# The order of the first loads of a two-block transformer kernel: modulation rows first, key weights ahead of the gate's third

## The chip, the cores and the metric

The kernel runs on one NeuronCore of a Trainium2 chip. The metric is the device time of one execution in microseconds (us). Before the change the median of three runs is 2579.94 us.

## What is computed

Two transformer-like blocks in fp32 on x of 1024 tokens by 1024 features. Only the start of the first one matters here:

```
mod = c @ w_ada + b_ada                       # c: 1 x 1024, w_ada: 1024 x 3072
shift, scale, gate = split(mod, 3)            # 1024 each
h = rmsnorm(x, norm_g) * (1 + scale) + shift
proj = h @ w_in                               # conv inputs, q, k, v (24 heads of 64), gates
q, k = partial_rope(q), partial_rope(k)       # needs tables of cos and sin by position
...                                           # conv branch, three dilated window attentions, merge
x = x + gate * (merged @ w_o)                 # gate is used here for the first time
```

A second block with its own attention, pooling branch and a feed-forward part follows; nothing of it is touched.

## The kernel before

**Precision.** A projection in fp32 is done as three matmuls: operands are split into an upper part (hi, fp32r) and the rest (lo), and hi*hi, hi*lo and lo*hi are summed in one PSUM bank. A unit of projection, such as ("k", 0, 3), that is key, head group 0, token block 3, is 8 k-steps of three 128 x 128 x 512 matmuls, 24 in all. Weights come as pieces of 128 x 512 (256 KB) through four buffers `raw`; POOL splits each into `w_hi` and `w_lo` (L1067, L1069). The order of the units is written out by `plan`; four PSUM banks take them in turn, and ACT or DVE empties each.

**Engines and queues.** Each engine has its own program and waits on semaphores. SP issues nearly all DMAs in the order of its program, so a DMA that must wait for a free buffer holds back all that stand behind it. The eight blocks of x are issued by ACT. POOL does the weight splits of the whole first part, in order.

**The opening.** w_ada comes as 48 pieces of 128 x 512, named (n, k): n is which sixth of the 3072 columns, k which 128 rows. n = 0, 1 are shift, 2, 3 are scale, 4, 5 the gate. `ADA` is the order in which they are loaded. Two ways are used to multiply by c:
- n = 0 and 2: DVE multiplies a piece by c's column and adds it up (`ada_sum`, L1546 and L1549) in `macc`; at the end PE sums over the partitions and turns the result into columns of `ps_s[0]` (`mod_cols`, L2329). This gives the first half of shift and scale, for `mod_half(0)` on DVE and so the first four feature tiles.
- n = 1 and 3 ("row pieces"): PE multiplies c's column by the piece (`mod_piece`, L2336) into a row of PSUM. ACT copies the two rows out (L1165), and PE turns them into columns of `ps_s[1]` (`row_cols`, L2343) after the first k-step of the projections, for `mod_half(1)`.
- n = 4 and 5 (the gate): DVE sums as above in `gacc`; `gate_rows` (L2367) makes a row of it on PE, DVE adds the bias row `mrow` (loaded at L707), and `gate_store` (L711) writes the row to DRAM.

The pieces pass through a ring of 10 buffers (the first 32), later of 6 (the gate's 16), and SP waits at a piece until the piece before it in its slot was used (`ada_piece`, L687). Eight query weight pieces are issued between them (`next_piece`, L650), four at once and then one per split of POOL. The ring lies in `vreg` and `late_hi`; V of the attention is later written to `vreg`.

Per token block B, PE transposes x, already scaled by DVE (L1535), into `featT` (L2323, two sets of four transposes, copied by ACT at L1134). Before the change the row pieces lag two blocks: PE turns block B and then multiplies the row pieces of B - 2; behind the loop stand `mod_cols` for n = 0 and 2, and the row pieces of the last two blocks. Then DVE applies shift and scale to a feature tile of 128 x 1024 (`h_affine`, L1571), ACT takes its upper part (L1125), DVE its lower part (L1529), and the projections begin: four query units together, k-step by k-step, then one at a time.

**Rotation.** Behind h DVE computes the angles, ACT two tables by Sin (L1168, L1169; semaphore `rope_tab`). For each query and key unit ACT copies the bank (L1129), DVE rotates (four operations, L1630 to L1633), and PE transposes the result (`turn`, L2323), behind the next unit.

**Order on SP before the change.** 32 pieces with the queries' weights between them, the 16 gate pieces, the bias row, then `qkv_io`: one prefetch of a weight piece of the next chunk per unit (query units prefetch key weights, key units value weights). DVE sums two gate pieces behind each query rotation, `gate_rows` stands behind key unit 2, DVE's bias addition behind key unit 4, `gate_store` behind key unit 6.

Of the kernel before, what the change touches and what calls it, by code (L numbers as in the profile page):

```python
# [27 lines left out]
NB = S // P  # L28
KT = D // P
# [10 lines left out]
POOL_W = (2, 4, 8, 16)  # L40
ACC = 4
LEAD = 4
ROW_LAG = 2
ADA = ([(n, k - (ROW_LAG if n in (1, 3) else 0)) for k in range(8 + ROW_LAG) for n in (0, 2, 1, 3)
        if 0 <= k - (ROW_LAG if n in (1, 3) else 0) < 8]
       + [(n, k) for n in (4, 5) for k in range(8)])
ADA_SUM = {key: i + 1 for i, key in enumerate([key for key in ADA if key[0] not in (1, 3)])}
ADA_ROW = {key: i + 1 for i, key in enumerate([key for key in ADA if key[0] in (1, 3)])}
RAW = 4
# [4 lines left out]
FIRST_ADA = 32  # L54
ADA_SLOT = [p % RING if p < FIRST_ADA else (p - FIRST_ADA) % RING2 for p in range(len(ADA))]
ADA_BEFORE = [[q for q in range(p) if ADA_SLOT[q] == ADA_SLOT[p]] for p in range(len(ADA))]

# [153 lines left out]
def build(nc, A, out):  # L211
# [8 lines left out]
    with ExitStack() as ctx:  # L220
# [3 lines left out]
        def sem(name):  # L224
            return ctx.enter_context(nc.semaphore(name))
# [141 lines left out]
        ada_used, ada_col = sem("ada_used"), sem("ada_col")  # L367
        ada_mm, row_out, gate_b = sem("ada_mm"), sem("row_out"), sem("gate_b")
        gate_mm, gate_sum, gate_st = sem("gate_mm"), sem("gate_sum"), sem("gate_st")
        gs_ready, h_aff = sem("gs_ready"), sem("h_aff")  # L370
        ang_ready, rope_tab = sem("ang_ready"), sem("rope_tab")
# [41 lines left out]
        def wait_unit(eng, u):  # L413

            eng.wait_ge(acc_ready, U[u] + 1)

        def wait_evac(eng, u):

            eng.wait_ge(acc_free[U[u] % ACC], U[u] // ACC + 1)
# [218 lines left out]
        def _(sp):  # L638
# [40 lines left out]
            def ada_piece(p):  # L679
                n, k = ADA[p]  # L680
                if ADA_BEFORE[p]:
                    old = ADA[ADA_BEFORE[p][-1]]
                    if old in ADA_ROW:
# [16 lines left out]
            for p in range(8, 32):  # L700
                ada_piece(p)
                if p in (14, 16, 18, 20, 22, 24, 26, 28):
                    next_piece()
            for p in range(32, 48):
                ada_piece(p)
            sp.wait_ge(ada_col, 3)
            sp.dma_start(mrow, A["b_ada_row"][:, 2 * D:3 * D]).then_inc(gate_b, 16)  # L707

            def gate_store():
                sp.wait_ge(gate_sum, 2)  # L710
                sp.dma_start(gate_row_d, mrow).then_inc(gate_st, 16)  # L711
# [84 lines left out]
            def qkv_io(g):  # L796
                for u in STAGE_QKV[g]:
                    prefetch(u)
                    conv_io(u)
                    if u == ("k", 0, 6):  # L800
                        gate_store()

            for g in range(NG):
# [41 lines left out]
            for u in STAGE_Z:  # L845
                if u[0] == "zc":
                    n = GATES.index(u)
# [54 lines left out]
            n = 0  # L902
# [99 lines left out]
            for n in range(PRODUCTS):  # L1002
                blk, q = n // 7, n % 7
# [113 lines left out]
        def _(act):  # L1117
# [9 lines left out]
            def copy_unit(u, dst):  # L1127
                wait_unit(act, u)
                nc.scalar.activation(dst, bank(u), ACT.Copy).then_inc(free_of(u), 1)  # L1129
# [41 lines left out]
            def qkv_unit(u):  # L1171
                name, g, B = u
                if name in "qk" and g < NG:
                    wait_slot(act, u)
                    copy_unit(u, slot(u))
                elif name == "v":
                    if B == 0 and g >= 1:
                        act.wait_ge(pv, 16 * g)
                    copy_unit(u, V[:, B, :])
                elif name in ("qt", "kt"):  # L1180
                    if g >= 1 and g < NG and name == "qt" and B == 0:
                        act.wait_ge(scores, 64 * g)
                    wait_unit(act, u)
                    if g in (1, 2):
                        dst = (qT if name == "qt" else kT)[:, :, :]
                        src = bank(u)
                        if g == 1:
                            dst = dst.rearrange("p k (r h j) -> p k r h j", r=4, h=2)[:, :, :, B // 4,
                                                                                     32 * (B % 4):32 * (B % 4) + 32]
                            src = src.rearrange("p (k j r) -> p k r j", k=4, r=4)  # L1190
                        else:
                            dst = dst.rearrange("p k (r j) -> p k r j", r=8)[:, :, :, 16 * B:16 * B + 16]
                            src = src.rearrange("p (k j r) -> p k r j", k=4, r=8)
                        nc.scalar.activation(dst, src, ACT.Copy).then_inc(free_of(u), 1)
                    elif g == 3 and name == "kt":
                        nc.scalar.activation(kT2[:, P * B:P * B + P], bank(u)[:, 0:P], ACT.Copy
                                             ).then_inc(free_of(u), 1)
                    else:
                        transposed(u, (qT if name == "qt" else kT)[:, :, P * B:P * B + P])
                elif name == "kv":  # L1200
                    wait_evac(act, u)
                    nc.scalar.activation(V2[:, B, :], slot(("k", 3, B))[:, P:2 * P], ACT.Copy
                                         ).then_inc(v2_out, 1)
# [88 lines left out]
            for u in STAGE_Z:  # L1292
                name, B, h = u
# [218 lines left out]
        def _(dve):  # L1512
# [194 lines left out]
            for g in range(NG):  # L1707
                if g:
                    dve.wait_ge(probs_t, 32 * g)
                else:  # L1710
                    dve.wait_ge(rope_tab, 2)
                for u in STAGE_QKV[g]:
                    if u[0] in "qk":
                        wait_evac(dve, u)
                        rotate(u, HPG)
                    conv_taps(u)
                    if u[:2] == ("q", 0):
                        for p in (32 + 2 * u[2], 33 + 2 * u[2]):
                            ada_sum(*ADA[p])
                    if u == ("k", 0, 4):  # L1720
                        dve.wait_ge(gate_mm, 1)
                        dve.wait_ge(gate_b, 16)
                        for h in range(2):
                            nc.vector.tensor_tensor(mrow[:, HALF * h:HALF * h + HALF], ps_s[h][0:1, :],
                                                    mrow[:, HALF * h:HALF * h + HALF], ALU.add
                                                    ).then_inc(gate_sum, 1)
                attention(g)
# [73 lines left out]
            for u in STAGE_Z:  # L1801
                name, B, h = u
# [154 lines left out]
            for u in unit_range(("q", 3, 0), ("kt", 3, 7)):  # L1957
                name, _, B = u
# [242 lines left out]
            for n in range(PRODUCTS):  # L2201
                blk, q = n // 7, n % 7
# [43 lines left out]
        def _(pe):  # L2246
# [86 lines left out]
            def mod_piece(n, k):  # L2333
                p = ADA.index((n, k))
                pe.wait_ge(ada_ld[ADA_SLOT[p]], 16 * (len(ADA_BEFORE[p]) + 1))
                nc.tensor.matmul(ps_row[n], small[:, k:k + 1], ada[ADA_SLOT[p]], start=(k == 0),  # L2336
                                 stop=(k == KT - 1)).then_inc(ada_mm, 1)
# [11 lines left out]
            for i in range(2):  # L2349
                nc.tensor.matmul(ps_s[i][:, 0:16], ident[:, :], b_mod, start=True, stop=False, skip_group_check=True)  # L2350
            for B in range(NB):
                pe.wait_ge(x_norm, B + 1)
                for h in range(2):
                    turn(("xt", B, h), [xs[B % XS][:, P * i:P * i + P] for i in range(4 * h, 4 * h + 4)])
                if B >= ROW_LAG:
                    for n in (1, 3):
                        mod_piece(n, B - ROW_LAG)
            mod_cols(0, ps_s[0])
            mod_cols(2, ps_s[0])
            for k in range(NB - ROW_LAG, KT):  # L2360
                for n in (1, 3):
                    mod_piece(n, k)

            def gate_rows():
                pe.wait_ge(ada_used, ADA_SUM[(5, 7)])
# [57 lines left out]
            def attention(g):  # L2423

                us = att_units(g)
                for r in range(16):
                    a, b, c, d = four_fill(len(ATT_STAGES[g]), r)
                    for m in range(a, b):
                        proj(us[m // 24], m % 24)
                    score_four(g, r)  # L2430
                    for m in range(b, c):
                        proj(us[m // 24], m % 24)
                    turn_four(g, r)
                    for m in range(c, d):
                        proj(us[m // 24], m % 24)
                    value_four(g, r)
# [8 lines left out]
            for g in range(NG):  # L2445
                for u in STAGE_QKV[g]:
                    if u not in lead:
                        qkv_unit(u)
                    if u == ("k", 0, 2):
                        gate_rows()  # L2450
                wait_evac(pe, ("v", g, 7))
                attention(g)

            def turn_attention(B):
# [3 lines left out]
            for u in STAGE_Z:  # L2458
                name, B, h = u
# [112 lines left out]
```

## Time and profile before

| | |
|---|---|
| median of 3 runs | 2579.94 us (2577.8 to 2580.2) |
| profiled execution | 2578.96 us, its span 2576.8 us |
| busy share of the span | PE 97%, DVE 60%, ACT 33%, POOL 26% |
| mean granted TensorE clock | 0.993 |

The profile is of one execution. The span runs from the first instruction of the program to the end of the last; the execution's own time lies 2.2 us above it. Engines: PE = TensorE, PEld = its weight loads, DVE = VectorE, ACT = ScalarE, POOL = GpSimd, SP = SyncE; a q behind the name is the engine's sequencer, which issues DMAs. L687 is line 687 of the kernel. Times within the span are from its start. Matmuls are pipelined: one of 128 x 512 is recorded with about 0.39 us, but they start 0.23 us apart.

### The profile page before, as it was taken

The page shows a single profiled execution, that of the slowest core. Times are in us where ns is not written, and L with a number is a line of the kernel's source. Part 1 is how long each engine was busy: PE and PEld are TensorE (multiplying, and loading weights), DVE is VectorE, ACT ScalarE, POOL GpSimd, SP SyncE. Part 2 cuts the span into 40 slices and gives each one's busy share as a digit, 9 for nine tenths or more (in the row PEclk, how much of TensorE's full clock was granted, in tenths as well). Part 3 has the DMA queues.
Part 4 walks back from the last instruction along what each step waited for, and adds up shares of the span by engine and source line. Part 5 has one row for each costly group of instructions (what it writes and reads, how often), then busy time and mean ns, then how long its engine had stood idle before and what let it go on. Part 6 is the DMA issues. An engine that isn't in the chain of part 4 may idle for free.

```text
span 2576.8 us, 31389 instructions
## 1 busy us (share of the span) xinstructions
PE 2498.2 (97%) x12016; PEld 2052.6 (80%) x12016; DVE 1555.6 (60%) x2476; ACT 854.0 (33%) x1664; POOL 674.8 (26%) x653
## 2 busy tenths in 40 slices
PE   7999999999999999989999999999999999999997
PEld 4787887887888887778888888887887788887876
DVE  7511348978778686565646521123557866858778
ACT  5213221122321232463114033231145545354553
POOL 3422224323244232322533332223310000000000
PEclk9999999999999999999999999999999999999999
DMA  7311212213231232633434122215449575666754
GB/s 254 103 49 46 71 64 61 71 42 99 83 94 48 75 97 77 220 103 131 131 132 140 30 86 74 74 66 176 137 121 294 129 190 154 166 193 163 193 127 105
DMA packets 162794, 300.83 MB, mean 117 GB/s; under 512 B 22098, under 2 KB 46418, under 8 KB 158804
## 3 DMA queue, kind: packets, MB, share of 16 engines
q1 hardware_dynamic: 142724, 250.05, 29.3%
q0 software_dynamic: 18768, 44.57, 9.5%
q10 hardware_dynamic: 1152, 4.19, 0.4%
q8 instruction: 96, 1.57, 0.2%
q14 instruction: 54, 0.44, 0.1%
HBM read 232.50 MB, written 57.87 MB: 113 GB/s over the span
## 4 chain that ended last, share of the span: by engine, by line
PE 79%; DVE 12%; DMA 2%; ACT 2%; issue 2%; POOL 1%; SPq 0%; DVEq 0%; ACTq 0%; POOLq 0%
PE ps L2294 52%; PE ps L2520 19%; DVE scr L1650 5%; PE ps L2418 3%; PE ps L2394 2%; PE ps L2404 2%; PE ps L2323 1%; DVE w_lo L2034 1%; DMA h2c_d<-late_hi 1%; DVE w_lo L2043 1%; DVE big L2092 1%; DMA vreg<-in_w_ada 1%; DVE scr L1630 0%; DVE big L1890 0%; DMA late_hi<-in_w_ada 0%
## 5 line engine op out<-in xcount | busy, mean ns | idle before, releaser
L2294 PE MATMUL ps<-act_hi,w_hi 128*128 128x512 f32 x1344 | 540.0, 402 | 13.5 <-DVE act_lo L1529 4.1
L1067 POOL CAST w_hi<-raw 128x512 fp32r<-128x512 f32 x288 | 216.1, 750 | 1224.4 <-DMA raw<-in_w_in 776.3
L2294 PE MATMUL ps<-act_lo,w_hi 128*128 128x512 f32 x1344 | 534.7, 398 | 0.0
L2294 PE MATMUL ps<-act_hi,w_lo 128*128 128x512 f32 x1344 | 527.1, 392 | 0.0
L1650 DVE SCALAR_TENSOR_TENSOR scr<-scr,small 128x512 f32<-128x512 f32 x480 | 431.9, 900 | 15.6
L1069 POOL TENSOR_TENSOR w_lo<-raw,w_hi 128x512 fp32r<-128x512 f32 x288 | 402.8, 1399 | 23.1
L2294 PE MATMUL ps<-w_hi,act_hi 128*128 128x512 f32 (+1 forms) x960 | 377.2, 393 | 4.3 <-POOL w_lo L1069 2.6
L2294 PE MATMUL ps<-w_hi,act_lo 128*128 128x512 f32 (+1 forms) x960 | 369.9, 385 | 0.0
L2294 PE MATMUL ps<-w_lo,act_hi 128*128 128x512 f32 (+1 forms) x960 | 369.2, 385 | 0.0
L2520 PE MATMUL ps<-w_hi 128*128 128x512 f32 x896 | 350.6, 391 | 10.8 <-issue 7.7
L2520 PE MATMUL ps<-w_hi,w_lo 128*128 128x512 f32 x896 | 349.4, 390 | 0.0
L2520 PE MATMUL ps<-w_lo,w_hi 128*128 128x512 f32 x896 | 349.3, 390 | 0.0
L2294 PEld LDWEIGHTS ps<-act_hi,w_hi 128*128 128x128 f32 x1344 | 254.2, 189 | 74.6 <-issue 15.9
L2294 PEld LDWEIGHTS ps<-act_lo,w_hi 128*128 128x128 f32 x1344 | 253.6, 189 | 57.0 <-issue 4.6
L2294 PEld LDWEIGHTS ps<-act_hi,w_lo 128*128 128x128 f32 x1344 | 253.9, 189 | 50.2
L2294 PEld LDWEIGHTS ps<-w_hi,act_hi 128*128 128x128 f32 x960 | 198.1, 206 | 34.4 <-POOL w_lo L1069 3.9
L2294 PEld LDWEIGHTS ps<-w_hi,act_lo 128*128 128x128 f32 x960 | 197.8, 206 | 31.0
L1233 ACT ACTIVATE scr<-scr,stat 128x256 f32<-128x256 f32 (+1 forms) x256 | 115.9, 454 | 319.4 <-DVE stat L1672 319.4
L2294 PEld LDWEIGHTS ps<-w_lo,act_hi 128*128 128x128 f32 x960 | 198.4, 207 | 28.4
L2520 PEld LDWEIGHTS ps<-w_hi 128*128 128x128 f32 x896 | 168.5, 188 | 50.7 <-issue 15.9
L2520 PEld LDWEIGHTS ps<-w_hi,w_lo 128*128 128x128 f32 x896 | 168.6, 188 | 35.1
L2520 PEld LDWEIGHTS ps<-w_lo,w_hi 128*128 128x128 f32 x896 | 168.6, 188 | 34.7
(235 smaller groups left out, 2682.3 us busy)
## 6 DMA issues: line engine op xcount, KB each, us to landing
raw<-in_w_in SPq DMA_DIRECT2D x176, 256.0 KB, 3.3
late_hi<-h2c_d SPq DMA_DIRECT2D x21, 1024.0 KB, 7.5
vreg<-in_w_ada SPq DMA_DIRECT2D x36, 256.0 KB, 5.3
raw<-in_w_in SPq DMA_DIRECT2D x72, 128.0 KB, 2.4
raw<-in_w_up POOLq DMA_DIRECT2D x8, 1024.0 KB, 12.0
late_lo<-in_w_up SPq DMA_DIRECT2D x8, 1024.0 KB, 5.4
late_lo<-in_w_up POOLq DMA_DIRECT2D x8, 1024.0 KB, 15.8
late_lo<-late_lo POOLq DMA_DIRECT2D x8, 1024.0 KB, 7.4
```

Source lines behind the costliest of these rows:

```text
L1067: pool.tensor_copy(dhi, src).then_inc(w_hi_done, 1)
L1069: pool.tensor_tensor(dlo, src, dhi.bitcast(F32), ALU.subtract).then_inc(w_ready, 1)
L1233: nc.scalar.activation(p_, p_, ACT.Exp, scale=-1.0, bias=stat[:, B, h:h + 1], accum_out=stat[:, B, 8 + h:9 + h]).then_inc(probs, 1)
L1650: nc.vector.scalar_tensor_tensor(ca, u_in[:, j:j + HALF], w[:, j:j + 1], ca, ALU.mult, ALU.add).then_inc(tap, 1)
L2034: nc.vector.tensor_tensor(lo[:, two, :], src[:, two, :], hi[:, two, :].bitcast(F32), ALU.subtract).then_inc(wc_lo, 1)
L2043: nc.vector.tensor_tensor(lo[:, two, :], src[:, two, :], hi[:, two, :].bitcast(F32), ALU.subtract).then_inc(ac_lo, 1)
L2092: nc.vector.tensor_tensor(dst[:, t, :], dst[:, t, :], bank_, ALU.add).then_inc(signal, 1)
L2294: ins = nc.tensor.matmul(out_, lhs, rhs, start=(m == 0), stop=(m == 3 * nk - 1))
L2394: nc.tensor.matmul(ps_s[j][:, 256 * e:256 * e + n], qT[rows, i, P * B:P * B + P], keys, start=True, stop=True).then_inc(scores, 1)
L2404: ins = nc.tensor.transpose(ps_s[j][:, cols], prob[j][:, cols], ident[:, :])
L2418: ins = nc.tensor.matmul(ps_o[:, P * e + HD * j:P * e + HD * j + HD], prob[j][:, 256 * e + P * i:256 * e + P * i + P], v, start=(i == 0), ...
L2520: ins = nc.tensor.matmul(ps[prod_bank(n, t)][:, :], lhs, rhs, start=(k == 0 and i == 0), stop=(k == 3 and i == 2))
```

## The change

The order of the pieces loses its lag and puts the two row pieces of a k first. On PE the row pieces of a block precede its transposes. SP issues only gate pieces 32 to 37 in the opening, then the bias row, then waits for the rope tables; the other ten gate pieces are issued behind the prefetches of the first five key units. DVE sums two gate pieces behind each key rotation. `gate_rows`, the bias addition and `gate_store` move to value units 2, 4 and 6. Two waits are new: ACT waits for the last sum before it writes V, and PE for the gate's sum before the first attention.

```diff
-ROW_LAG = 2
-ADA = ([(n, k - (ROW_LAG if n in (1, 3) else 0)) for k in range(8 + ROW_LAG) for n in (0, 2, 1, 3)
-        if 0 <= k - (ROW_LAG if n in (1, 3) else 0) < 8]
+ADA = ([(n, k) for k in range(8) for n in (1, 3, 0, 2)]
        + [(n, k) for n in (4, 5) for k in range(8)])
...
@@ SP
                 ada_piece(p)
                 if p in (14, 16, 18, 20, 22, 24, 26, 28):
                     next_piece()
-            for p in range(32, 48):
+            for p in range(32, 38):
                 ada_piece(p)
             sp.wait_ge(ada_col, 3)
             sp.dma_start(mrow, A["b_ada_row"][:, 2 * D:3 * D]).then_inc(gate_b, 16)
+            sp.wait_ge(rope_tab, 2)
...
                     prefetch(u)
                     conv_io(u)
-                    if u == ("k", 0, 6):
+                    if u[:2] == ("k", 0) and u[2] < 5:
+                        ada_piece(38 + 2 * u[2])
+                        ada_piece(39 + 2 * u[2])
+                    if u == ("v", 0, 6):
                         gate_store()
@@ ACT, qkv_unit
                         act.wait_ge(pv, 16 * g)
+                    if B == 0 and g == 0:
+                        act.wait_ge(ada_used, ADA_SUM[(5, 7)])
                     copy_unit(u, V[:, B, :])
@@ DVE
-                    if u[:2] == ("q", 0):
+                    if u[:2] == ("k", 0):
                         for p in (32 + 2 * u[2], 33 + 2 * u[2]):
                             ada_sum(*ADA[p])
-                    if u == ("k", 0, 4):
+                    if u == ("v", 0, 4):
                         dve.wait_ge(gate_mm, 1)
                         dve.wait_ge(gate_b, 16)
@@ PE
             for B in range(NB):
+                for n in (1, 3):
+                    mod_piece(n, B)
                 pe.wait_ge(x_norm, B + 1)
                 for h in range(2):
                     turn(("xt", B, h), [xs[B % XS][:, P * i:P * i + P] for i in range(4 * h, 4 * h + 4)])
-                if B >= ROW_LAG:
-                    for n in (1, 3):
-                        mod_piece(n, B - ROW_LAG)
             mod_cols(0, ps_s[0])
             mod_cols(2, ps_s[0])
-            for k in range(NB - ROW_LAG, KT):
-                for n in (1, 3):
-                    mod_piece(n, k)
...
-                    if u == ("k", 0, 2):
+                    if u == ("v", 0, 2):
                         gate_rows()
                 wait_evac(pe, ("v", g, 7))
+                if g == 0:
+                    pe.wait_ge(gate_sum, 2)
                 attention(g)
```

## Rows read from the trace of the kernel before

**Rows 1.** The page: the chain that ended last, shares by engine.
```profile
PE 79%; DVE 12%; DMA 2%; ACT 2%; issue 2%; POOL 1%; SPq 0%; DVEq 0%; ACTq 0%; POOLq 0%
```

**Rows 2.** Stages: length, busy us by engine, granted PE clock, DMA share, GB/s.
```profile
10.00:20.00 10.00, 5.84 (x25) 3.66 (x24) 5.71 (x11) 7.37 (x15) 0.00 (x0) 0.80 1.05 368
...
30.00:40.00 10.00, 7.67 (x30) 2.44 (x29) 9.39 (x12) 3.29 (x7) 9.68 (x9) 1.00 1.05 387
```

**Rows 3.** Timeline of SP, 37 to 82 us: start, length, instructions merged.
```profile
37.24 44.63 SPq L687 DMA_DIRECT2D vreg<-in_w_ada  x18
```

**Rows 4.** Line 687, the issue at 37.7 us: lengths in ns, starts, landing.
```profile
L687 SPq DMA_DIRECT2D vreg<-in_w_ada x1: 430/430/430, 37.7 to 37.7; - x1
...
DMA to landing us min/median/max: 5.5/5.5/5.5
```

**Rows 5.** Timeline of PE, 9 to 47 us; brackets: idle before, releaser.
```profile
9.43 3.48 PE L2323 MATMUL ps<-ident,scr 128*128 128x128 f32 x16 [3.27 <-DVE scr L1535]
...
18.44 3.57 PE L2336 MATMUL ps<-late_hi,small 128*1 128x512 f32 x4 [1.74 <-DMA late_hi<-in_w_ada]
...
35.62 1.09 PE L2323 MATMUL ps<-ident,scr 128*128 128x128 f32 x8
...
39.70 1.95 PE L2329 MATMUL ps<-small,vreg 128*128 128x1 f32 x16
...
43.29 1.88 PE L2336 MATMUL ps<-vreg,small 128*1 128x512 f32 x4
46.78 0.47 PE L2294 MATMUL ps<-w_hi,act_hi 128*128 128x512 f32 x1 [1.61 <-DVE act_lo L1529]
```

**Rows 6.** Chain of waits, 41 to 47 us: start, length, what.
```profile
41.95 1.48 DVE big L1571
43.45 1.07 ACT act_hi L1125
44.54 2.10 DVE act_lo L1529
```

**Rows 7.** Timeline of DVE, 46 to 49 us.
```profile
46.55 0.80 DVE L1571 TENSOR_SCALAR big<-big,col 128x1024 f32<-128x1024 f32 x1
47.27 1.22 DVE L1529 TENSOR_TENSOR act_lo<-big,act_hi 128x1024 fp32r<-128x1024 f32 x1
```

**Rows 8.** Chain of waits, 80 to 120 us.
```profile
80.76 0.77 DVE scr L1549
...
82.29 4.63 DMA raw<-in_w_in
...
102.50 1.60 POOL w_lo L1069
...
105.31 0.85 PE ps L2323 x4
106.17 6.44 PE ps L2294 x24
112.61 0.44 PE ps L2323 x4
113.05 5.47 PE ps L2294 x24
118.52 1.81 PE ps L2367 x4
```

**Rows 9.** Timeline of PE, 94 to 96 us.
```profile
95.52 0.60 PE L2323 MATMUL ps<-ident,scr 128*128 128x128 f32 x4
```

**Rows 10.** Waits on PE, 86 to 113 us: total us, times, longest.
```profile
PE ps L2294 <- POOL w_lo L1069: 2.6, 2, 1.7
```

**Rows 11.** Timeline of ACT, 67 to 69 us.
```profile
67.75 0.40 ACT L1169 ACTIVATE cosT<-scr 128x256 f32<-128x256 f32 x1
```

**Rows 12.** Timeline of DVE, 90 to 97 us: first rotation operation, two sums.
```profile
90.50 0.54 DVE L1630 TENSOR_TENSOR scr<-scr,cosT 128x128 f32<-128x128 f32 x1 [3.37 <-ACT scr L1129]
...
93.55 2.82 DVE L1549 SCALAR_TENSOR_TENSOR scr<-vreg,small,scr 128x512 f32<-128x512 f32 x2
```

## The prediction

> **What bounds the kernel now.** I read four views: the page with its chain of waits, the table of stages, then the chain and the timelines of the first 120 us, since every edit lies there. The page puts 79% of the chain on PE [rows 1]: past the opening the work is a train of matmuls, and whatever removes idle PE time ahead of it, or adds some, moves the end by the same amount. So two places matter.
>
> *The opening, 0 to 46.8 us.* The DMA engines are full, 368 GB/s from 10 to 20 us and 387 from 30 to 40 [rows 2]. A 256 KB piece then takes 262144 B / 387 GB/s = 0.68 us, and pieces land one behind another. SP hands the last modulation pieces and all the gate's pieces to the queue in one stretch of 18 from 37.24 on, 44.63 us long [rows 3]. The last modulation piece ahead of the gate's third is issued at 37.7 and is 5.5 us under way, so it lands at 43.2 [rows 4]. Yet PE forms the columns of shift and scale at 39.70 [rows 5], before the last pieces have landed: they are row pieces, which only the second half of the columns needs. From there it is DVE's affine, ACT's upper part (1.07), DVE's lower part (2.10), and the first projection at 46.78 after 1.61 us of idle PE [rows 5, 6].
>
> *The key weights, 80 to 113 us.* In that stretch of SP's queue the gate pieces from the seventh on wait for a slot that a sum beside a query rotation frees, and the key weights stand behind them. The chain shows it: a sum on DVE at 80.76, the first key piece in flight from 82.29 for 4.63, POOL's splits from then to 104.10, and only then the last matmuls of the first key unit. Behind it the clock fell to its lower level, 1.2 GHz: four transposes took 0.85 instead of 0.44 us, and a unit of 24 matmuls 6.44 instead of 5.47 [rows 8].
>
> **Part 1: key weights are asked for behind the rope tables.** SP now issues gate pieces only up to the sixth, loads the bias row, waits for the two tables and then prefetches keys. The second table is written by 68.15 [rows 11]; with the opening's shift (part 3) that is 70.2. The first key piece then needs 2.5 to 4.6 us (4.63 is the one row of it, with four pieces in the queue) and is in by 75. Eight splits took 104.10 - 86.92 = 17.2 us with a busy DVE beside them, so the last is ready by 92. The first key unit is due at 96.1 + 2.3 = 98.4: 6 us to spare, the stall is gone whole. Its size: from the transposes behind the last query unit at 95.52 [rows 9] to the third key unit at 113.05 is 17.53 us. The work in it is three transposes of 0.44 and two units of 5.47, as the next ones run [rows 8]: 12.26. So **-5.3 us**, the low clock included. Bounds: -2.6 (only PE's two waits for POOL [rows 10]) to -5.3. I take the full value, since the gap between the two is short gaps at the same matmuls and the low clock behind them.
>
> What it adds: POOL's splits now run from 75 to 92 under the query rotations. A rotation beside POOL took 93.55 - 90.50 = 3.0 us, with the first sum right behind it [rows 12]. Each has a unit of 5.47 us as cover from its copy to its transpose, and the sums are gone from beside it. The first, which has no such cover, comes at about 72, before POOL starts. Price nothing; if the cover failed, up to 3.0 us per unit.
>
> **Part 2: the gate's sums move beside the key rotations, the gate's row into the value units.** Sixteen sums leave the query stretch, where they were not on PE's path except through SP, and join the keys: rotation 3.0 + two sums 2.82 = 5.8 us with POOL active throughout [rows 12], against a unit's period of 5.91. POOL has only one value piece per key unit (1.9 us), so about 4 us of 5.9. SP is new in this stretch: behind each of the first five key prefetches it waits for that unit's sums before it can ask for the next value piece. The fifth key unit ends at 98.4 + 4 x 5.91 + 5.5 = 127.5, its sums at latest 6.4 later, 133.9; the last three value pieces, with two gate pieces ahead of them, land some 5 us later, by 139, and take 3 x 2.15 = 6.5 on POOL, 145.5. The first value unit starts at 98.4 + 8 x 5.91 = 145.7, and needs its last piece only 4.8 us later. Covered. ACT's first copy into V now waits for the last sum, at most 6.4 us behind the last key unit against 5.9 for the value unit itself: 0.5 us late on one of four banks, free. The two gate matmuls cost PE 1.81 us where they stand [rows 8], between key units before, between value units after: the same. The wait for the gate's sum ahead of attention is met units earlier. Part 2 is **0**; bounds 0 to +3.5 (the value weights as late as the keys' were, 9.0 for a unit of 5.47).
>
> **Part 3: the opening.** All eight input blocks load the same bytes, and the SP waits that hold issues back from 24 us on are on POOL's splits, whose places in the queue are unchanged. So I let the last piece land at 43.2 again. But it is now the second scale piece, on which DVE's sum, and with it the first columns, depend, and the two row pieces before it stand ahead of the last block's transposes on PE. Two chains:
> - DVE: 43.2 + sum 0.77 + columns of one piece 1.95 / 2 = 45.0.
> - PE: the second row piece lands two pieces before the last, 43.2 - 2 x 0.68 = 41.8; its matmul 1.88 / 2, the two sets of transposes 1.09, both columns 1.95 [rows 5]: 45.8.
>
> The later one counts: 45.8, against 39.70 + 1.95 = 41.65 now, 4.1 us later. Part of it comes back: from 46.5 on affine and lower part took 0.80 and 1.22 [rows 7], against 1.48 and 2.10 for the first ones, which ran beside POOL's last query splits [rows 6]. Mine come behind those splits: 45.8 + 0.3 + 0.80 + 1.07 + 1.22 + 0.1 = 49.3, against 46.78: +2.5. POOL too may be quicker where DVE waits for pieces, and then the pieces land up to 1 us sooner: half of that off. **+2.0 us**; bounds +0.8 to +3.6 (all of it off and no contention; DVE and POOL slowing each other as now).
>
> **Part 4: the clock at the start.** PE now idles from 45.8 to about 49. Before, it idled 1.61 us there and the clock stayed at 2.4 GHz, by the first matmul's 0.47 [rows 5]; behind the 2.6 us of waits around 103 [rows 10] it fell, and cost 0.41 + 0.97 [rows 8] and some 0.3 at the matmuls ahead of these, 1.7 in all. My idle is longer than either, but of a kind seen once each way: even chances at 1.7 us, **+0.9**; bounds 0 to +3.4 (it falls twice).
> The Trainium skill, page "TensorE: Matmul & The Clock Gate", section "HAM oscillation — how this bites in real kernels", says that a wait for data between bursts re-throttles the array and the next burst begins cold, each time anew. By it the sum would be 0.8 us higher than by the row of 46.78, at which a short wait cost nothing.
>
> **Sum.** -5.3 + 0 + 2.0 + 0.9 = -2.4. The profiled execution took 2578.96 us, of which the span is 2576.8: 2576.6. The median of the runs shown is 1.0 above that execution, so 2577.5 beside it. Of the chances: a change under 0.2% (5.2 us) can't be told from none with this kernel.
>
> **Rivals.**
> 1. *The opening costs nothing* (13%). The row pieces, now spread over all blocks, keep the clock up, DVE is idle more often, POOL gets ahead, and the last pieces land two us sooner. For it: PE ran at 0.80 of its clock from 10 to 20 us [rows 2]. Against: the DMA engines are full, whatever the order. It gives -5.3 + 0.1: 2574.7.
> 2. *PE becomes the bound of the opening* (6%). If the clock stays at its lower level, a row pair takes 3.57 and a block's transposes 3.48 / 2 [rows 5], 5.3 us per block on PE, and each now blocks the next; DMA needs 5 x 0.68 = 3.4. The third block's first row piece lands 31 pieces before the last, 43.2 - 31 x 0.68 = 22.1; six blocks from there end at 53.9, the columns at 55.9, the first projection 3.5 later at 59.4, +12.6. That would be 2579.9 - 5.3 + 12.6 = 2587.2, slower than before. It decides if the clock is low for more than 5 of the 8 blocks; before, it was at 1.00 from 30 us on.
> 3. *The value weights are late* (4%), because SP waits for sums five times. If DVE is beside POOL all the time they come up to 3.5 us late: 2581. Against: the margin above is 5 us, and it starts from worst durations.
> 4. *The keys are still late* (2%), the change not doing what it says: the tables would have to be 6 us later. Some 2580.
>
> **Chances and range.** Forecast 75%. Its own range is 2575.5 to 2580, from the bounds of parts 3 and 4. Rival 1 takes in 2574.5, rivals 3 and 4 2581; 2574.2 to 2581.8 leaves rival 2 and the far half of rival 1 outside. Faster by over 0.2% means under 2574.8: half of rival 1 and the low end of the forecast, 13%. Slower by over 0.2% means above 2585.1: rival 2, and stalls that I have not seen, 7%.
>
> **What would show it.** Part 1: key pieces issued at about 70, POOL's splits between 73 and 92, no PE idle ended by POOL between 90 and 115, and the clock at full there. Part 2: sums between key rotations, value splits ending before 146, no PE wait at the first value unit. Part 3: columns at about 44 to 46 and the first projection at 48 to 50; if it starts at 46.8 or sooner, part 3 is wrong and rival 1 holds. Part 4: the clock in the first 4 us of the projections. The whole forecast is wrong if the span moves by more than the shift of the third key unit's start, for then something behind 113 us changed too.

## The result

The changed kernel is slower: median 2588.06 us of 20 runs (2579.7 to 2592.95) against 2579.49 us of 20 runs (2577.01 to 2581.26). The ratio over all runs is 1.0027, 95% interval 1.0020 to 1.0033, that is 5.2 to 8.5 us; the medians alone lie 8.6 us apart, because the runs of the changed kernel bunch at two ends. The forecast was 2577.5 us, in a range from 2574.2 to 2581.8. The spread has grown as well, from 4 to 13 us: five of the 20 runs lie at 2579.7 to 2581.3, three at 2582.8 to 2583.0, twelve at 2585.5 and above. The profiled execution took 2589.3 us, so it is one of the long ones.

The stages of the changed kernel, with the columns of [rows 2]: PE is busy 4.68 of the 10 us from 40 on and 5.55 of those from 80 on, and in the stage behind each gap the granted clock is 0.67 and 0.75 on average, that is at its lower level, 1.2 GHz, for a part of the stage.

```profile
30.00:40.00 10.00, 7.34 (x29) 2.16 (x27) 7.85 (x11) 5.77 (x12) 9.68 (x9) 1.00 1.05 387
40.00:50.00 10.00, 4.68 (x29) 3.57 (x29) 8.82 (x15) 4.22 (x7) 6.01 (x5) 0.86 0.59 192
50.00:60.00 10.00, 10.00 (x38) 7.96 (x38) 7.29 (x10) 3.96 (x4) 0.00 (x0) 0.67 0.00 0
...
80.00:90.00 10.00, 5.55 (x29) 4.28 (x28) 9.79 (x12) 1.70 (x4) 9.52 (x12) 0.90 0.38 105
90.00:100.00 10.00, 10.00 (x38) 8.25 (x39) 2.60 (x8) 1.69 (x3) 1.12 (x1) 0.75 0.00 0
```

PE's timeline of the changed kernel, beside [rows 5]. The columns of shift and scale come 2.6 us later, the first projection 2.4 us later, behind 4.97 us of idle PE instead of 1.61. Its matmuls are recorded with 0.63 us and stand 0.43 us apart where the ones of full clock have 0.39 and 0.23. Then PE waits three times for a rotation, 5.5 us in all.

```profile
42.29 1.96 PE L2333 MATMUL ps<-small,vreg 128*128 128x1 f32 x16
49.21 0.76 PE L2298 MATMUL ps<-w_hi,act_hi 128*128 128x512 f32 x1 [4.97 <-DVE act_lo L1533]
49.78 0.63 PE L2298 MATMUL ps<-w_lo,act_hi 128*128 128x512 f32 x1
50.20 0.63 PE L2298 MATMUL ps<-w_hi,act_lo 128*128 128x512 f32 x1
...
78.23 0.66 PE L2327 MATMUL ps<-ident,scr 128*128 128x128 f32 x4 [1.07 <-DVE scr L1637]
86.04 0.66 PE L2327 MATMUL ps<-ident,scr 128*128 128x128 f32 x4 [1.24 <-DVE scr L1637]
89.90 1.12 PE L2327 MATMUL ps<-ident,scr 128*128 128x128 f32 x4 [3.21 <-DVE scr L1637]
```

The reason is on the timelines of DVE and POOL: the key splits begin at 75.44, just ahead of the first rotation, and last to 91. A rotation then takes 3.9 us, from 86.01 to 89.85.

```profile
75.86 0.34 DVE L1634 TENSOR_TENSOR scr<-scr,cosT 128x128 f32<-128x128 f32 x1 [3.82 <-ACT scr L1131]
...
86.01 1.39 DVE L1634 TENSOR_TENSOR scr<-scr,cosT 128x128 f32<-128x128 f32 x1
87.32 0.69 DVE L1635 TENSOR_TENSOR scr<-scr,sinT 128x128 f32<-128x128 f32 x1
88.05 1.24 DVE L1636 TENSOR_TENSOR scr<-scr 128x64 f32<-128x64 f32 x1
89.22 0.63 DVE L1637 TENSOR_TENSOR scr<-scr 128x64 f32<-128x64 f32 x1
```
```profile
75.44 0.61 POOL L1069 CAST w_hi<-raw 128x512 fp32r<-128x512 f32 x1 [29.27 <-DMA raw<-in_w_in]
...
89.85 1.27 POOL L1071 TENSOR_TENSOR w_lo<-raw,w_hi 128x512 fp32r<-128x512 f32 x1
```

Here is the chain of waits of the changed kernel, beside [rows 8]. It runs over the rotations up to 89.86, then one unit at the lower clock (7.38 us for what takes 5.47), then unit by unit with no stall. The unit at 122.52 is the third key unit, which stood at 113.05.

```profile
89.22 0.64 DVE scr L1637
89.86 0.04 issue
89.90 1.12 PE ps L2327 x4
91.02 7.38 PE ps L2298 x24
98.40 0.44 PE ps L2327 x4
98.83 5.47 PE ps L2298 x24
...
122.52 5.48 PE ps L2298 x24
```

The sum at that unit, in the two profiled executions (before, the first query block is transposed at 70.72 and the sixth query unit starts at 78.11):

| step | us |
|---|---|
| first projection later, 49.21 - 46.78 | +2.4 |
| four joint query units, end at 78.23 - 1.07 = 77.16 against 70.72, less the above | +4.0 |
| to the sixth query unit, 91.02 against 78.11, less the two above: waits for rotations 1.07 + 1.24 + 3.21, and slow transposes | +6.5 |
| one query unit at the lower clock, 7.38 - 5.47 | +1.9 |
| stall of the keys gone | -5.3 |
| sum; the third key unit, 122.52 - 113.05 | +9.5 |

At the first attention it is 9.6 us (PE's first matmul behind the emptying of the last value unit at 204.87, before at 195.24), so the stretch between takes as long as before to 0.2 us. At the end of the span it is 10.7. The 1.1 us more lie behind the first attention, which the change does not touch, and the table at the end of the experiments shows that this part differs by up to 8.6 us from one profiled execution to another.

### The profile page after: what moved, and what is told of

Read it like the earlier page. It is cut to its first block, busy times and chain, and to the rows that moved or that the text cites. A ratio compares the mean times of both kernels' runs of the same rounds, so it can differ in the third digit from the quotient of the medians.

```text
span 2587.5 us, 31393 instructions
## 1 busy us (share of the span) xinstructions
PE 2504.0 (97%) x12016; PEld 2055.9 (79%) x12016; DVE 1557.2 (60%) x2476; ACT 852.1 (33%) x1664; POOL 677.9 (26%) x653
## 4 chain that ended last, share of the span: by engine, by line
PE 79%; DVE 13%; ACT 3%; issue 2%; DMA 2%; SPq 1%; DVEq 0%; ACTq 0%
PE ps L2298 52%; PE ps L2522 19%; DVE scr L1654 5%; PE ps L2418 3%; PE ps L2394 2%; PE ps L2404 2%; PE ps L2327 1%; DVE w_lo L2038 1%; DVE scr L1634 1%; DMA h2c_d<-late_hi 1%; DVE w_lo L2047 1%; DVE big L2096 1%; DMA late_hi<-in_w_ada 0%; DVE scr L1637 0%; DVE big L1894 0%
## 5 line engine op out<-in xcount | busy, mean ns | idle before, releaser
L2298 PEld LDWEIGHTS ps<-w_hi,act_lo 128*128 128x128 f32 x960 | 198.8, 207 | 31.7
```

The source lines that it names most:

```text
L2298: ins = nc.tensor.matmul(out_, lhs, rhs, start=(m == 0), stop=(m == 3 * nk - 1))
```

## The experiments

Theory A says that there are two separate losses: the later opening with a low clock behind it, and POOL's splits under rotations that have no cover. Rival B says that the opening alone is the cause, and that the waits at the rotations follow from it. Rival C says that the low clock has nothing to do with idle PE. Each kernel was run beside the kernel before, whose median was 2579.93 beside the first four, 2579.0 beside the next four and 2578.66 beside the last two.

**e1, opening of before.** The edit takes back the order of `ADA` and PE's loop, and nothing else:

```diff
-ADA = ([(n, k) for k in range(8) for n in (1, 3, 0, 2)]
+ROW_LAG = 2
+ADA = ([(n, k - (ROW_LAG if n in (1, 3) else 0)) for k in range(8 + ROW_LAG) for n in (0, 2, 1, 3)
+        if 0 <= k - (ROW_LAG if n in (1, 3) else 0) < 8]
```

> The changed kernel with the opening of before (order of the pieces, PE's loop); key weights still asked for behind the rope tables. Theory A (two costs: the later start of the projections with a low clock behind it, 6.3 us; and key splits under the first four query rotations, three of which have one unit's cover between them, 5.5 us idle and 2.6 of low clock): 2579.5 - 5.3 + 8.1 = 2582, first projection at 46.8, PE waiting some 5 us for rotations between 70 and 85. Rival B (all of the loss is the opening, the waits at the rotations follow from it): 2574.

Measured: 2578.52 us, ratio 0.9997 (0.9988 to 1.0005). That is between the two numbers, and the twelve runs spread from 2575.45 to 2584.58. The first projection starts at 46.50, as said, but PE waits for a rotation only once, 1.7 us:

```profile
PE ps L2329 <- DVE scr L1639: 1.7, 1, 1.7
PE ps L2300 <- DVE act_lo L1535: 1.4, 1, 1.4
```

On DVE's timeline the first two rotations come before POOL's splits or just at their start (70.53) and take 0.9 and 1.2 us; the third and fourth need 3.8:

```profile
69.31 0.29 DVE L1636 TENSOR_TENSOR scr<-scr,cosT 128x128 f32<-128x128 f32 x1 [2.19 <-ACT scr L1133]
...
71.44 1.27 DVE L1636 TENSOR_TENSOR scr<-scr,cosT 128x128 f32<-128x128 f32 x1
...
78.44 0.63 DVE L1639 TENSOR_TENSOR scr<-scr 128x64 f32<-128x64 f32 x1
```

The last of the four ends at 79.07, and PE's transposes follow at 79.12. So the second loss is not a fixed 8 us: it depends on the first, and so far B is right. B's 2574 is missed too: a wait is left with the old opening.

**e2, key weights behind the fourth rotation.** The new opening is kept:

```diff
-            sp.wait_ge(rope_tab, 2)
+            sp.wait_ge(roped, 4)
```

> The changed kernel, but SP asks for the key weights behind the fourth query rotation and not behind the rope tables; its own opening is kept. Theory A: the rotations run alone, 1 us each, PE's waits for them go, 2588 - 8 = 2580; the last key split comes before the first key unit, so nothing is lost there. Rival B: 2588, the waits stay.

Measured: 2581.73 us, ratio 1.0009 (1.0000 to 1.0017). By the medians it is 6.3 us below the changed kernel, by the two ratios 4.6, and at the first attention its trace is 8.4 us ahead (196.47 against 204.87). The second rotation in it takes 0.9 us; these are its first and last operation on DVE's timeline:

```profile
76.86 0.29 DVE L1634 TENSOR_TENSOR scr<-scr,cosT 128x128 f32<-128x128 f32 x1
...
77.53 0.22 DVE L1637 TENSOR_TENSOR scr<-scr 128x64 f32<-128x64 f32 x1
```

All that PE still waits for between 46 and 115 us is the start; no wait for POOL appears, so the keys are in time even so:

```profile
PE ps L2298 <- DVE act_lo L1533: 4.9, 1, 4.9
```

B is out as the whole cause: it wanted 2588.

**e3, both edits.**

> Both edits: opening of before, key weights behind the fourth query rotation. Theory A: the whole stall of 5.3 us is gained and nothing paid, 2579.5 - 5.3 = 2574. Rival B: 2574 as well. If the gate's sums in the key stretch cost something that neither names, it is above 2576.

Measured: 2575.55 us, ratio 0.9987 (0.9979 to 0.9996); faster than both kernels. By the medians 4.4 of the 5.3 us of the key stall are gained, by the interval 1.0 to 5.4. The chain of waits is sharper. The third key unit starts 5.2 us sooner than before (113.05):

```profile
107.85 5.48 PE ps L2300 x24
```

The first attention starts 5.0 us sooner (190.20 against 195.24), so what was moved into the key and value units costs 0.2 us between the two in this execution. PE's waits between 46 and 115 us are one line:

```profile
PE ps L2300 <- DVE act_lo L1535: 1.7, 1, 1.7
```

And e2 against e3 prices the opening where the rest is clean: 2581.73 - 2575.55 = 6.2 us by the medians, 196.47 - 190.20 = 6.3 by the traces.

**e4, the new opening alone** on the kernel before.

> The kernel before with the new order of pieces and PE's new loop alone; gate pieces and key weights as before. Theory A: projections 2.4 us later, 3.9 of low clock behind 5 us of idle PE, 2579.5 + 6.3 = 2586. The prediction's part 3 and 4: +2.9, 2582.4. Rival B: +8 or more, 2588.

Measured: 2584.70 us, ratio 1.0023 (1.0014 to 1.0032): 4.8 us over before. That is nearer to A's 6.3 than to the prediction's 2.9, and short of both B and A. The start, on PE's timeline, was at 49.78:

```profile
49.78 0.76 PE L2292 MATMUL ps<-w_hi,act_hi 128*128 128x512 f32 x1 [4.23 <-DVE act_lo L1527]
```

The trace shows where A's sum is lost again. The first query block is transposed at 76.91 against 70.72, 6.2 us later, as A has it. The third key unit starts at 117.16 against 113.05, only 4.1 later: PE waits for the keys' splits as before (2.5 us against the 2.6 of [rows 10]), but here the granted clock stays at 1.00 through that stall, which in the kernel before it did not.

**e5, PE kept busy**, on e2: five fp32 matmuls into the bank that the first projection then overwrites.

```diff
             lead = [("q", 0, B) for B in range(LEAD)]
+            begin(lead[0])
+            for _ in range(5):
+                nc.tensor.matmul(bank(lead[0]), ident[:, :], macc[0], start=True, stop=True)
```

> e2 (new opening, key weights behind the fourth rotation) with five fp32 matmuls of 128x512 more on PE ahead of the first projection, some 0.94 us each, in the 4.9 us in which PE idled there; their result is overwritten. Theory A (the low clock behind the idle stretch costs some 3.9 us): the first projection starts as before at 49.3 or up to 0.5 later, its matmuls come 0.23 us apart, and the run takes 2581.7 - 3.5 = 2578. Rival C (the clock's low stretches fall where they will and idle PE has nothing to do with it; the loss of the opening is something else): 2581.7 to 2582.2.

Measured: 2579.21 us, ratio 0.9999 (0.9990 to 1.0007). The median is 2.5 us below e2's though the kernel does more work, but the intervals of the two ratios overlap. The stages tell more; first e2:

```profile
46.00:51.00 5.00, 1.70 (x4) 1.44 (x5) 4.60 (x6) 4.01 (x5) 0.26 (x1) 0.62 0.55 195
51.00:56.00 5.00, 5.00 (x24) 3.96 (x23) 3.13 (x4) 1.06 (x1) 0.00 (x0) 0.70 0.00 0
56.00:61.00 5.00, 5.00 (x18) 4.02 (x18) 4.17 (x7) 2.43 (x3) 0.00 (x0) 0.66 0.00 1
```

and e5:

```profile
46.00:51.00 5.00, 5.00 (x9) 2.10 (x8) 4.56 (x8) 3.49 (x5) 0.35 (x1) 0.66 0.76 254
51.00:56.00 5.00, 5.00 (x29) 3.88 (x27) 3.69 (x4) 1.59 (x2) 0.00 (x0) 1.00 0.00 2
56.00:61.00 5.00, 5.00 (x17) 4.02 (x18) 4.20 (x7) 2.45 (x3) 0.00 (x0) 0.66 0.00 1
```

The clock is low in both from about 46 us on, though in e5 PE idles no longer than 0.62 us: what stands ahead of it there are the one-column matmuls of the columns, in two groups with that gap between. But without the idle time it is at full again from 51 on, where in e2 it averages 0.70, that is the lower level for some 60% of the stage. The added matmuls ran at 1.2 GHz themselves, 6.24 us instead of 4.7, and pushed the first projection from 49.30 to 51.15. Gain and cost cancel: the first query block is transposed at 77.04 in e5 and at 77.08 in e2, and the first attention starts at 196.52 and 196.47. So the low clock behind the idle stretch cost some 1.9 us here, not 3.9, and the 2.5 us between the medians are not explained by these two traces.

C is out by the traces and not by the time. In the five profiled kernels in which PE idled 3.7 to 5.0 us ahead of the first projection (the changed one, e2, e4, e7, e9) the projections began at the lower level; in the five with 1.7 us or less (before, e1, e3, e8, e10) they began at full, and so they did, but for their first matmul, in e5 and e6, where the gap was filled. Theory A is only part of it. The third stage is low in e2 and e5 alike, behind the sixteen one-column matmuls of `row_cols`, and e6 and e10 below show that this second fall comes and goes on its own.

**e6, the same five matmuls on the changed kernel.**

> The changed kernel itself with the same five matmuls. Theory A: the four joint query units end some 3.9 us earlier, so that the first rotations come before POOL's key splits and not under them; as in e1 one wait of about 1.7 us for a rotation is left instead of 5.5, so two losses shrink: 2588.1 - 3.9 - 4 = 2580. If the two costs are independent of one another: 2588.1 - 3.9 = 2584. Rival C: 2588.

Measured: 2585.52 us, ratio 1.0015 (1.0005 to 1.0026), but in two groups: five of twelve runs from 2576.8 to 2580.9, seven from 2584.8 to 2588.5. The profiled execution, 2579.4 us, is of the lower group, and has the single wait:

```profile
84.20 0.66 PE L2327 MATMUL ps<-ident,scr 128*128 128x128 f32 x4 [1.74 <-DVE scr L1637]
```

Its projections run at full clock, and not only at the start. Behind `row_cols`, where e5 with the same opening fell to 0.66, it stays at 1.00:

```profile
51.00:56.00 5.00, 5.00 (x28) 3.79 (x26) 3.76 (x4) 1.66 (x2) 0.00 (x0) 1.00 0.00 1
56.00:61.00 5.00, 5.00 (x24) 4.20 (x24) 4.10 (x7) 2.36 (x3) 0.00 (x0) 1.00 0.00 1
```

The first query block is transposed 1.5 us sooner than in e5 for it (75.52 against 77.04), and again two rotations come ahead of most of the splits. At the first attention this execution is 8.0 us ahead of the changed kernel's, close to A's 3.9 + 4. The upper group was not profiled. That its query units end later and so meet the splits with all four rotations is argued and not shown; the part behind the first attention took 2380.7 us here and up to 2387.7 in other profiled kernels, which would nearly be enough by itself.

**e7, no wait for the tables**: the same line as in e2 is removed, nothing put in its place.

> The changed kernel without SP's wait for the rope tables: key weights are asked for at about 57, behind the bias row, and POOL splits them from 59 to 75, beside DVE's lower parts and the rope tables. Theory A (DVE and POOL slow each other wherever they meet): DVE's table chain of some 12 us grows by 5 or more, the first rotation starts at about 79 instead of 75.9, but rotations then run alone at 1 us each; PE waits 2 to 4 us once: 2585. If splits cost DVE only in the rotations: 2588 - 8 = 2580.

Measured: 2592.54 us in five runs, ratio 1.0049 (1.0037 to 1.0061), the slowest of all. DVE and POOL slow each other in the table chain as well: eight operations of 128x32, 0.80 us together in the changed kernel, took 3.91 us, and PE waited 8.6 us for the first rotations.

```profile
72.71 3.91 DVE L1610 TENSOR_SCALAR scr<-scr 128x32 f32<-128x32 f32 x8
```
```profile
PE ps L2326 <- DVE scr L1636: 8.6, 1, 8.6
PE ps L2297 <- DVE act_lo L1532: 3.7, 1, 3.7
```

Theory A's direction holds, but its 2 to 4 us of waiting are less than half of the 8.6. The wait for the tables is worth having; it only ends too early.

**e9, only POOL's work moved**: SP asks for the keys as in the changed kernel, the splits start behind the fourth rotation. Only the first four pieces fly under the rotations; the other four need a buffer that a split frees.

```diff
                 if c >= 2 and s == 0:
                     pool.wait_ge(acc_ready, U[chunk_last[c - 2]] + 1)
+                if c == 1 and s == 0:
+                    pool.wait_ge(roped, 4)
```

> The changed kernel; SP asks for the key weights as it does there, so that their transfers run under the first rotations, but POOL begins to split them only behind the fourth rotation. If it is POOL's work that slows the rotations: no wait of PE for a rotation, 2582, as e2. If it is the transfers or SP's order: 2588, as the changed kernel.

Measured: 2581.40 us, ratio 1.0012 (1.0003 to 1.0021), e2's time, and no wait of PE for a rotation. From 75 to 80 us the DMA engines moved 195 GB/s, in the changed kernel 198, and the rotations took 0.9 us each. So it is POOL's splits that slow them, and not the transfers.

**e8, row pieces lag three blocks**: e3 with `ROW_LAG = 3`, a step away from the change and past the kernel before.

> e3 (opening of before, key weights behind the fourth rotation) with the row pieces lagging three blocks instead of two. Theory A (the first columns wait for whatever stands ahead of them in the order of pieces and on PE): the columns start up to 1.5 us sooner than 39.7, the first projection at 45.5 to 46, 2575.5 - 1 = 2574.5. If DVE is the limit there: 2575.5, unchanged.

Measured: 2573.86 us, ratio 0.9971 (0.9961 to 0.9982), the lowest median of all, 5 us below the kernel before. Its interval just overlaps e3's; at the first attention its trace is 1.9 us ahead of e3's (188.28 against 190.20). On PE's timeline the columns start at 37.75, the row pieces of three blocks fill the time that affine and split take, and the first projection follows at 44.87 with no idle time:

```profile
37.75 1.95 PE L2335 MATMUL ps<-small,vreg 128*128 128x1 f32 x16
39.62 3.59 PE L2342 MATMUL ps<-late_hi,small 128*1 128x512 f32 x8
43.05 1.88 PE L2342 MATMUL ps<-vreg,small 128*1 128x512 f32 x4
44.87 0.50 PE L2300 MATMUL ps<-w_hi,act_hi 128*128 128x512 f32 x1
```

**e10, a lag of four.**

> e3 with a lag of four blocks for the row pieces. DVE's last pieces come two places sooner still, but eight row matmuls of 0.94 us then stand between the columns and the first projection; in e8 with six it began at 44.9 without idle PE. If the row work is now the limit: columns at about 37, first projection at 46, 2575. If not: 2573.

Measured: 2574.53 us, ratio 0.9982 (0.9973 to 0.9991). Columns start at 35.84 and the first projection at 44.45, only 0.4 us sooner than with three: PE's eight row matmuls, two for each of four blocks, now end last there. The time is not told apart from e8's. In the trace the lead is lost again: the clock falls behind `row_cols` (47.40), although PE had not idled since 35.84, and the first query block is transposed at 70.03, in e8 at 68.86.

```profile
46.00:51.00 5.00, 5.00 (x29) 4.16 (x28) 4.84 (x7) 2.10 (x3) 0.00 (x0) 0.90 0.73 252
51.00:56.00 5.00, 5.00 (x19) 4.02 (x18) 4.60 (x6) 3.07 (x3) 0.00 (x0) 0.75 0.00 0
```

**All profiled executions at the first attention.** One execution of each kernel was profiled. The second column is the start of PE's first matmul behind the emptying of the last value unit, the third its distance from the kernel before, the fourth what is left of the span, and the last the distance of the medians (each from the kernel before beside it).

| kernel | at the first attention | against before | rest of the span | medians |
|---|---|---|---|---|
| before | 195.24 | | 2381.6 | |
| changed | 204.87 | +9.6 | 2382.6 | +8.6 |
| e1 | 191.75 | -3.5 | 2386.3 | -1.4 |
| e2 | 196.47 | +1.2 | 2387.7 | +1.8 |
| e3 | 190.20 | -5.0 | 2382.1 | -4.4 |
| e4 | 199.40 | +4.2 | 2386.2 | +4.8 |
| e5 | 196.52 | +1.3 | 2379.1 | +0.2 |
| e6 | 196.82 | +1.6 | 2380.7 | +6.5 |
| e7 | 209.25 | +14.0 | 2382.0 | +13.5 |
| e8 | 188.28 | -7.0 | 2384.7 | -5.1 |
| e9 | 195.53 | +0.3 | 2382.9 | +2.7 |
| e10 | 189.49 | -5.8 | 2386.9 | -4.1 |

The rest, in which no edit changes anything, takes 2379.1 to 2387.7 us. What moves it is open. So single executions can be compared in the opening and not at the end, and differences of 2 or 3 us between medians are not to be leaned on.

## Why the prediction was wrong

**Part 1, its gain: right.** It said that the keys would be ready by 92 and the stall gone. The last split ended at 91.1, PE waited for none, and in e3 the third key unit comes 5.2 of the 5.3 us sooner.

**Part 1, its price: the step that failed.** It set the rotations beside POOL at 3.0 us each and their cost at nothing, since "Each has a unit of 5.47 us as cover from its copy to its transpose". It cost 8.4 us, the +6.5 and +1.9 of the table above. Three things in it were wrong. The plan has the transposes of the second, third and fourth query block stand together behind one unit, so that three rotations, 11.7 us at 3.9 each, share a cover of 5.47. The code said so: `plan` collects them in `late`, and in the trace of before the transposes at 76.63 are twelve in a row. The row for 3.0 us was a favourable one: its first operation took 0.54 us, while the next rotation of the same trace (96.41 to 100.14) took 3.7. And the first rotation was to come "at about 72, before POOL starts": with the clock low in the joint units it came at 75.86, 6.3 us later than before (69.58), while the tables, from which SP counts, had moved by only 4.6 us. Without the splits beside the rotations the trace is 8.4 us (e2) and 9.3 us (e9) ahead at the first attention, the medians 6.3 and 6.7. The prediction did name the price, up to 3.0 us per unit if the cover failed, but gave it no place in its sum, its range or its rivals; rival 3 looked for a new wait in the key stretch.

**Part 2: right in its result.** Value splits were done at 154.3, ahead of the first value unit at 158.06, and PE waited for nothing between 100 and 200 us. Both times are later than the 145.5 and 145.7 forecast, with everything else. In e3 the stretch from the third key unit to the first attention takes 0.2 us longer than before.

**Part 3: right in size, partly by luck.** The first projection was to start 2.0 to 2.5 us later and started 2.4 later, but two errors cancel in it. The columns were predicted 4.1 us later and came 2.6 later: PE was done with them at 44.25 and not at 45.8. From there to the first projection it took 4.97 us and not the 3.5 reckoned. The prediction let PE's columns end last; in fact it was DVE, which behind its last two sums still had five small operations on constants to do up to 45.0, 1.23 us the first of them, and then ran its first affine beside POOL in 1.56 us instead of 0.80.

**Part 4: the mis-sized term.** It allowed 0.9 us as the mean of none and one low stretch, 1.7 us each. The joint units lost 4.0 us, past the upper bound of 3.4, over two low stretches, one up to 54 us that cost 2.2 (the first twelve matmuls took 5.20 us against 2.97) and one from 57 us on that cost the rest. The idle time was 4.97 us where 3.2 were reckoned. Only the first of the two stretches belongs to it: in e5 and e6, without idle time, the clock was at full from 51 us on, and the second came in e5 and not in e6. The section "HAM oscillation — how this bites in real kernels" of the page "TensorE: Matmul & The Clock Gate" of the Trainium skill, cited there, says that behind a wait for data the next burst begins cold. The trace agrees for the waits of 4.97 us and of 3.21 us (ahead of 89.90, behind which a unit took 7.38 us), and not for those of 1.07 and 1.24 us ahead of them, behind which the clock stayed at 1.00. Where the prediction says that the sum would by this section be 0.8 us higher than by the row of 46.78, it is 0.8 higher than with the +0.9 that it took; by that row alone the term is nothing, and the difference 1.7.

**The sum.** -5.3 + 2.4 + 4.0 for the known terms would have been +1.1, about 2580.6, still inside the range; the rotations bring the rest. The five shortest runs of the changed kernel, 2579.7 to 2581.3, lie near that figure. None of them was profiled. Their spans are 2577.9 to 2579.5 us, and even with the shortest rest seen, 2379.1, their first attention would have started by 198.8 to 200.4, some 4.5 to 6 us sooner than in the profiled execution. That is an estimate, and which part of the two losses they were spared is not shown. Rival 2 gave 2587.2, close to the median, but by a mechanism that did not occur: it had the first projection at 59.4, and it started at 49.21.

## What to carry to other kernels

When work is moved to an engine's idle stretch, look at what its neighbour does there in its shortest instructions, and count how many of them share one cover before the next consumer, in the written order of the units and not by the average. Order the pieces of a load by what the first dependent step needs and put independent PE work behind it, not ahead: here that is a lag of three blocks, the opposite of the change. A gap on PE costs its length. From the first projection to the third key unit, a stretch at half clock came behind every gap of 3.2 us and more as well; behind the gaps of 1.7 us and less it came once (before, around 103 us), and not behind the same stall in e4. Filling the gap with work that has to be done anyway (e8) gained 1.9 us over e3 at the first attention; filling it with nothing useful (e5) gained nothing there. And when two times differ by a few us out of 2580, compare the traces up to the last place that the edit touches, before the rest of the kernel adds its own spread.

## What the hardware showed

- A short DVE operation beside POOL's splits can take about as long as one POOL instruction, whatever its size: 128x64 took 0.22 us alone and up to 1.27 beside it, 128x128 0.28 and up to 1.40, and POOL's own instructions are 0.61 and 1.27 us long. The longer sums of 128x512 only doubled, from 0.77 to 1.4 ([rows 8, 12]). Chains of many short operations suffer most: 0.80 to 3.91 us in e7.
- Behind the sixteen one-column matmuls of `row_cols`, 1.9 us between two stretches of large ones, a stretch at 1.2 GHz followed in six of the twelve profiled executions (changed, e2, e4, e5, e7, e10) and not in the other six (before, e1, e3, e6, e8, e9). e5 and e6 have the same opening and differ in it, and in e10 it came with no idle PE ahead. What decides it is open.
- The same program can fall into two groups of times some 8 us apart (e6), and the part of this kernel that no edit touched took 2379.1 to 2387.7 us. A median alone says little here.
